# Chunk tables of a scan mixer: products formed in the stored layout instead of being transposed packet by packet

## The reference, cut to what matters

```python
lam_bar = jnp.exp(lam * dt)
b_bar = ((lam_bar - 1.0) / lam)[..., None] * lax.complex(b_re, b_im)
bu = einsum('bsgp,gnp->bsgn', u, b_bar)         # u: [512, 64 groups, 16]
hs = associative_scan(a1*a2, a2*x1 + x2)        # h[t] = lam_bar*h[t-1] + bu[t]
y  = einsum('gpn,bsgn->bsgp', c, hs).real       # forward + backward, + d_skip*u
```

## Time and profile before

| | |
|---|---|
| runs, device time | 2927.89, 2930.91 (median), 2933.01 us |
| profiled execution, its own time | 2930.03 us |
| its span | 2928.2 us |
| PE busy | 2796.3 us, 95% of the span, 15552 products |
| PEld busy | 2277.3 us, 78% |
| DVE busy | 1570.8 us, 54% |
| ACT busy | 1134.6 us, 39% |
| POOL busy | 339.3 us, 12% |
| instructions | 38710 |

### The profile page before, as it was taken

How to read it: one execution, slowest core, us unless ns; L and a number is a source line. 1 busy time by engine, 2 the same in 40 slices (tenths; PEclk the granted TensorE clock), 3 DMA queues, 4 the chain that set the end, 5 groups by cost and what they waited for, 6 DMA issues and landing times. The chain is left out here.

```text
span 2928.2 us, 38710 instructions
## 1 busy us (share of the span) xinstructions
PE 2796.3 (95%) x15552; PEld 2277.3 (78%) x15552; DVE 1570.8 (54%) x2341; ACT 1134.6 (39%) x1792; POOL 339.3 (12%) x426
## 2 busy tenths in 40 slices
PE   9999999599999999999999899999999999999887
PEld 8788888488888877777788578888988888776665
DVE  7776664754434434554535654344654344664656
ACT  5332232364222324645647342223432123543443
POOL 0333221710000001111112300000000000110100
PEclk9999999799999999999999799999999999999989
DMA  4245557554444223222222323222222222211101
GB/s 142 96 147 170 156 155 222 192 160 120 130 127 116 96 75 110 70 92 80 87 94 91 126 101 101 101 88 103 69 101 89 99 100 101 82 49 40 57 15 46
DMA packets 116020, 307.08 MB, mean 105 GB/s; under 512 B 28176, under 2 KB 73808, under 8 KB 87296
## 3 DMA queue, kind: packets, MB, share of 16 engines
q1 hardware_dynamic: 108064, 278.39, 29.0%
q10 hardware_dynamic: 6336, 21.76, 2.1%
q0 software_dynamic: 1440, 4.46, 0.5%
HBM read 266.91 MB, written 41.85 MB: 105 GB/s over the span
## 5 line engine op out<-in xcount | busy, mean ns | idle before, releaser
L94 PE MATMUL ps<-hh_,wh_ 128*128 128x512 f32 x2184 | 867.2, 397 | 8.8 <-DVE hl_ L135 5.1
L94 PE MATMUL ps<-hh_,wl_ 128*128 128x512 f32 x2184 | 853.9, 391 | 0.0
L94 PE MATMUL ps<-hl_,wh_ 128*128 128x512 f32 x2184 | 853.7, 391 | 0.0
L121 DVE TENSOR_TENSOR wl_<-raw_,wh_ 128x2048 fp32r<-128x2048 f32 (+4 forms) x245 | 483.2, 1975 | 503.6 <-ACT wh_ L117 503.1
L117 ACT ACTIVATE wh_<-raw_ 128x2048 fp32r<-128x2048 f32 (+3 forms) x244 | 400.6, 1648 | 351.6 <-PE ps L94 331.2
L94 PEld LDWEIGHTS ps<-hh_,wh_ 128*128 128x128 f32 x2184 | 412.2, 189 | 107.0 <-issue 9.3
L94 PEld LDWEIGHTS ps<-hh_,wl_ 128*128 128x128 f32 x2184 | 411.9, 189 | 87.4
L94 PEld LDWEIGHTS ps<-hl_,wh_ 128*128 128x128 f32 x2184 | 412.4, 189 | 86.2 <-issue 2.9
L94 PE MATMUL ps<-ah_,wh_ 128*128 128x512 f32 x704 | 275.1, 391 | 0.0
L94 PE MATMUL ps<-al_,wh_ 128*128 128x512 f32 x704 | 274.0, 389 | 0.0
L94 PE MATMUL ps<-ah_,wl_ 128*128 128x512 f32 x704 | 274.0, 389 | 0.0
(11 more groups left out here) (363 smaller groups left out, 3584.5 us busy)
## 6 DMA issues: line engine op xcount, KB each, us to landing
raw_<-in_w SPq DMA_DIRECT2D x203, 1024.0 KB, 5.0
sO<-s5ce_ SPq DMA_DIRECT2D x32, 256.0 KB, 3.7
sW<-s5wt_ SPq DMA_DIRECT2D x16, 512.0 KB, 6.0
sA<-os_ SPq DMA_DIRECT2D x24, 256.0 KB, 2.1
ol_<-sA SPq DMA_DIRECT2D x24, 256.0 KB, 3.6
sT<-sK SPq DMA_DIRECT2D x32, 128.0 KB, 4.0
wh_<-sO ACTq DMA_DIRECT2D x4, 1024.0 KB, 6.1
wl_<-sO ACTq DMA_DIRECT2D x4, 1024.0 KB, 7.5
```

The lines of the kernel that those rows point to most:

```text
L94: return self.e.matmul(out, lhsT, rhs, start=start, stop=stop, skip_group_check=True)
L121: return Nothing() if self.e is None else self.e.tensor_tensor(out, a, b, op)
```

## The change

- The eight transposes of every packet go, with the two ACT copies behind them. Instead `P.G` is transposed once (eight transposes, two ACT copies), written to HBM (`sG`, 512 KB), and for each packet eight DMAs of 64 KB spread the packet's powers over the partitions in the layout of sW (`chunk_sync`; in the trace's terms `s5G_<-sG`). One more table from the host (`s5bt`, 512 KB a packet, to `P.bx`, `s5bx_`) has b in that layout. The x = 1 part is then formed from these and goes into `P.wt` as it is stored.
- What PE needs of `wn` for sK are two powers per state only. POOL forms these in six operations of 128x64 for each packet (`scaled_b`), from `P.fb`, a copy of the first power that DVE makes once. PE now waits for `p.wn` in place of `p.f(pc, 1)`.
- A packet takes nine slots in place of eight. DVE starts packet pc in slot 27 + 9pc, PE forms its products in slot 32 + 9pc: packet 13 in slot 149, packets 14 and 15 in what would be slots 158 and 167, past the 153 of FFN 0.

The core of the diff:

```diff
+    for _ in range(PREP_FIRST + 2):
+        yield
+    sp.wait_ge(*K.at("p.gt", 1))
+    sp.dma(d["sG"].rearrange("r b q n -> q (r b) n"), P.flat.rearrange("p (b n) -> p b n", b=8)).then_inc(*K.lane("s5sG").up("p.sG"))
+    yield
+    sp.wait_ge(*K.at("p.w"))
+    sp.dma(P.bx[:, :, :], d["s5bt"][0]).then_inc(*K.lane("s5gx").up())
+    sp.wait_ge(*K.at("p.sG"))
+    chunk_sync(K, sp, 0, range(8))
+    yield
+    for pc in range(16):
+        yield
+        if pc % 4 == 0 and pc:
+            same_sync(K, sp, pc // 4 - 1)
         yield
...
+        sp.wait_ge(*K.at("p.f", pc, 1))
+        sp.dma(d["sW"][un][:, 1024 * hf:1024 * hf + 1024], P.flat).then_inc(*K.lane("s5sW").up("p.sW", pc))
         if pc < 15:
-            sp.wait_ge(*K.at("p.f", pc, 1))
+            sp.wait_ge(*K.at("p.wn", pc))
             sp.dma(P.bc[:, :, :, :], d["s5bc"][pc + 1]).then_inc(*K.lane("s5bc").up("p.bc", pc + 1))
-        yield
-        yield
+            sp.dma(P.bx[:, :, :], d["s5bt"][pc + 1]).then_inc(*K.lane("s5gx").up())
+        yield
+        if pc < 15:
+            chunk_sync(K, sp, pc + 1, range(4))
+        yield
+        if pc < 15:
+            chunk_sync(K, sp, pc + 1, range(4, 8))
         yield
...
+def chunk_sync(K, sp, pc, powers):
+
+    for i in powers:
+        sp.dma(K.prep.G[16 * i:16 * i + 16, :, :, :].rearrange("p r s g -> p r (s g)"),
+               bass.AP(K.d["sG"].tensor, 512 * pc + 8192 * i, [[0, 16], [65536, 2], [1, 512]])).then_inc(
+            *K.lane("s5gx").up(*(("p.gx", pc) if i == 7 else ())))
...
+    for r in range(2):
+        ac.wait_ge(*K.at("p.gp", r))
+        ac.act(P.flat[:, 512 * r:512 * r + 512], K.mb["p.gp", r], ACT.Copy).then_inc(*ac.up("p.gt", r))
+        ac.mark("out", "p.gp", r)
+    yield
+    yield
...
-        yield
-        if pc:
-            ac.wait_ge(*K.at("p.sW", pc - 1))
-        for r in range(2):
-            ac.wait_ge(*K.at("p.t", pc, r))
-            ac.act(P.wt[:, :, r, :], K.mb["p.t", pc, r].rearrange("p (g x) -> p g x", g=4), ACT.Copy).then_inc(*ac.up("p.wt", pc, r))
-            ac.mark("out", "p.t", pc, r)
-        yield
+        for _ in range(4):
+            yield
...
-    for _ in range(4):
+    for _ in range(8):
         yield
     dv.wait_ge(*K.at("p.G"))
+    dv.cp(P.fb[:, :, :], pw[:, :, 0, :]).then_inc(*dv.up("p.fb"))
     for pc in range(16):
         for x in range(2):
-            out = (P.ce, P.wn)[x]
+            out = P.ce[:, 0, :, :, :], P.wt[:, :, 0, :]
...
-            dv.wait_ge(*K.at("p.bc", pc))
+            dv.wait_ge(*K.at(("p.bc", "p.gx")[x], pc))
...
+            if x:
+                dv.wait_ge(*(K.at("p.sW", pc - 1) if pc else K.at("p.sG")))
+            elif pc:
+                dv.wait_ge(*K.at("p.ab", pc - 1))
+                dv.wait_ge(*K.at("p.sO", pc - 1, 1))
...
-            dv.tt(out[:, 0, :, :, :], v[0], v[1], ALU.subtract).then_inc(*dv.up("p.o0", pc, x))
+            dv.tt(out[x], v[0], v[1], ALU.subtract).then_inc(*dv.up("p.o0", pc, x))
...
+def scaled_b(K, po, pc):
+
+    P = K.prep
+    t = [P.t2[:, 512 + 64 * i:576 + 64 * i].rearrange("p (g x) -> p g x", g=4) for i in range(2)]
+    fr, fi = (P.fb[:, r, 4 * pc:4 * pc + 4].rearrange("p (g x) -> p g x", x=1).broadcast_to([128, 4, 16]) for r in range(2))
+    br, bi = P.bc[:, 0, :, :], P.bc[:, 1, :, :]
+    po.wait_ge(*K.at("p.fb"))
+    for r, (x, y, op) in enumerate(((br, bi, ALU.subtract), (bi, br, ALU.add))):
+        po.tt(t[0], x, fr, ALU.mult).then_inc(*po.up())
+        po.tt(t[1], y, fi, ALU.mult).then_inc(*po.up())
+        if r == 0 and pc:
+            po.wait_ge(*K.at("p.ab", pc - 1))
+        po.wait_ge(*po.now())
+        po.tt(P.wn[:, r, :, :], t[0], t[1], op).then_inc(*po.up(*(("p.wn", pc) if r else ())))
+        po.wait_ge(*po.now())
...
 def prep_tensor(K, pe):
     P = K.prep
     ce, wn = P.ce, P.wn
-    for _ in range(PREP_FIRST):
+    for _ in range(PREP_FIRST + 1):
+        yield
+    pe.wait_ge(*K.at("p.G"))
+    for r in range(2):
+        b = K.mb.take("p.gp", r)
+        pe.wait_ge(*K.after(pe, K.mb, "p.gp", r))
+        for i in range(4):
+            m = pe.tr(b[:, 128 * i:128 * i + 128], P.gx[:, r, 128 * i:128 * i + 128], K.ident)
+        m.then_inc(*pe.up("p.gp", r))
+    for _ in range(3):
         yield
     for pc in range(16):
-        for _ in range(6):
+        for _ in range(4):
             yield
...
-        pe.wait_ge(*K.at("p.f", pc, 1))
+        pe.wait_ge(*K.at("p.wn", pc))
         for r in range(2):
             for g in range(4):
                 o = slice(32 * g, 32 * g + 16)
-                pe.mm(ba[o, 0:128], wn[0:64, r, g, 7, :], ce[0:64, r, g, 0:8, :], r == 0, r == 1).then_inc(*pe.up())
-                pe.mm(bb[o, 0:128], wn[64:128, r, g, 0, :], ce[64:128, r, g, 2:10, :], r == 0, r == 1).then_inc(*pe.up())
+                pe.mm(ba[o, 0:128], wn[0:64, r, g, :], ce[0:64, r, g, 0:8, :], r == 0, r == 1).then_inc(*pe.up())
+                pe.mm(bb[o, 0:128], wn[64:128, r, g, :], ce[64:128, r, g, 2:10, :], r == 0, r == 1).then_inc(*pe.up())
         pe.mark("p.ab", pc)
-        yield
-        for r in range(2):
-            b = K.mb.take("p.t", pc, r)
-            pe.wait_ge(*K.after(pe, K.mb, "p.t", pc, r))
-            for g in range(4):
-                m = pe.tr(b[:, 128 * g:128 * g + 128], wn[:, r, g, :, :].rearrange("p s x -> p (s x)"), K.ident)
-            m.then_inc(*pe.up("p.t", pc, r))
-        yield
+        for _ in range(5):
+            yield
...
-    e.wait_ge(*K.at("p.t", 15, 1))
+    e.wait_ge(*K.at("p.ab", 15))
+    e.wait_ge(*K.at("p.f", 15, 1))
     e.wait_ge(*K.at("p.sO", 15, 1))
```

More of the change, by code:

```diff
@@ L933, in prep_sync @@
     sp.dma(P.bc[:, :, :, :], d["s5bc"][0]).then_inc(*K.lane("s5bc").up("p.bc", 0))
-    for _ in range(PREP_FIRST):
+    for _ in range(PREP_FIRST + 2):
         yield
-    for pc in range(17):
-        if pc:
[L938 to L945, removed]
+    sp.wait_ge(*K.at("p.gt", 1))
[7 more added lines that the diff above has]
+    for pc in range(16):
         yield
+        if pc % 4 == 0 and pc:
+            same_sync(K, sp, pc // 4 - 1)
         yield
@@ L988, in prep_scalar @@
     ac.act(u[5], u[1], ACT.Sin, scale=0.5).then_inc(*ac.up("p.s2"))
-    for _ in range(PREP_FIRST - 2):
+    for _ in range(PREP_FIRST):
         yield
+    for r in range(2):
[4 more added lines that the diff above has]
+    yield
     for pc in range(16):
-        for _ in range(6):
+        for _ in range(5):
             yield
@@ L1099, in prep_vector @@
             if x == 0:
-                dv.stt(out[:, 1, :, :, :].rearrange("p g s x -> p (g s x)"), P.t1[:, 0:n], -1.0, P.t2[:, 0:n],
+                dv.stt(P.ce[:, 1, :, :, :].rearrange("p g s x -> p (g s x)"), P.t1[:, 0:n], -1.0, P.t2[:, 0:n],
                        ALU.mult, ALU.subtract).then_inc(*dv.up("p.f", pc, x))
             else:
-                dv.tt(out[:, 1, :, :, :], v[0], v[1], ALU.add).then_inc(*dv.up("p.f", pc, x))
+                dv.tt(P.wt[:, :, 1, :], v[0], v[1], ALU.add).then_inc(*dv.up("p.f", pc, x))
             yield
-        yield
         yield
@@ L1113, in prep_vector @@
         yield
+        yield
+        yield
     yield
 def prep_views(P, pc, x):
[L1118 to L1122, removed]
-    return n, v, er, ei, xr, xi
+    if x:
+        v = [t[:, 0:512].rearrange("p (g n) -> p g n", g=4) for t in (P.t1, P.t2)]
+        tabs = [t[:, r, :].rearrange("p (g n) -> p g n", g=4) for t in (P.gx, P.bx) for r in range(2)]
+        return 512, v, *tabs
+    n = 640
+    v = [t.rearrange("p (g s x) -> p g s x", g=4, s=10) for t in (P.t1[:, 0:n], P.t2[:, 0:n])]
+    er, ei = (P.E[:, r, :, 4 * pc:4 * pc + 4].rearrange("p s (g x) -> p g s x", x=1).broadcast_to([128, 4, 10, 16]) for r in range(2))
+    xr, xi = (P.bc[:, r, :, :].rearrange("p g (s x) -> p g s x", s=1).broadcast_to([128, 4, 10, 16]) for r in (2, 3))
+    return n, v, er, ei, xr, xi
+def scaled_b(K, po, pc):
[12 more added lines that the diff above has]
+        po.wait_ge(*po.now())
 def prep_gpsimd(K, po):
@@ L3839, in _s5 @@
     bc = np.ascontiguousarray(np.stack(b, 1).transpose(2, 0, 1, 3, 4))
+    bt = np.stack(b[:2]).reshape(2, 128, 16, 4, 16).transpose(2, 4, 0, 3, 1).reshape(16, 1, 16, 2, 512)
+    bt = np.broadcast_to(bt, (16, 8, 16, 2, 512)).reshape(16, 128, 2, 512)
     ds = np.zeros((4, 32, 16, 16), np.float32)
@@ L4015, in memory @@
         P.pw = P.ce[:, :, :, :, :].rearrange("p r g s x -> p (r g s x)")[:, 0:1152].rearrange("p (r k g) -> p r k g", r=2, k=9)
-        sm = P.wn[:, :, :, :, :].rearrange("p r g s x -> p (r g s x)")[:, 0:512].rearrange("p (k g) -> p k g", k=8)
-        P.u = [sm[:, i, :] for i in range(8)]
-        P.lr, P.li, P.dt = (P.wn[:, 1, i, :, :].rearrange("p s x -> p (s x)")[:, 0:64] for i in range(3))
+        P.u = [P.bx[:, 0, 64 * i:64 * i + 64] for i in range(8)]
+        P.lr, P.li, P.dt = (P.bx[:, 1, 128 * i:128 * i + 64] for i in range(3))
+        P.gx = P.G[:, :, :, :].rearrange("p r s g -> p r (s g)")
```

(5 more changed lines are left out.)

16 lines of the change are left out of this document (4 added, 12 removed).

## The result

The changed kernel takes 2976.8 us (median of four runs, 2969.4 to 2982.2) beside 2931.0 before: ratio 1.016, interval 1.014 to 1.018. Slower, as forecast, but by 46 us where 19 were forecast, and outside the range. The profiled execution has a span of 2967.6 us, 39.4 more than before. The whole loss arises before the scan: PE's first output product stands at 630.6 us in place of 582.9, +47.7. Some 8 us come back much later, in stretches that the change doesn't touch: of the same work, 1200 to 1300 us had a granted clock of 0.93 before and (47.7 us later) 0.97 after. Such clock differences come and go between executions, and the other three runs lie higher than the profiled one.

The account below looks back on a forecast made before the run. PE was taken to bound FFN 0, a chain of transfers and small operations the part behind it. FFN 0 saves 14.6 less 3 us, yet the first scaled U comes 18.6 later: 2930.0 + 18.6 = 2949 us, range 2937 to 2963.

Parts of the forecast that it names:

- What FFN 0 saves: PE in FFN 0: transposes, two packets' products and stream restarts go, one transpose set comes back; 14.6 us saved.
- What FFN 0 loses: Hold-ups of PE in FFN 0, at the start and through DVE waiting for POOL; 3 us together.
- the second: DVE in FFN 0 stands for POOL's six operations per packet, mostly covered by spare time; 0 to 10 us, 2 taken.
- the first: Start of FFN 0: copies, sG's write, nine DMAs and POOL's operations before packet 0's products; 0 to 5 us, 1 taken.
- What stands behind FFN 0: Packets 14 and 15, then U, from the last add at 478.0 to the first scaled U at 518.3.
- The first parts: x = 0 part of packets 14 and 15: two rounds of POOL's 1.34 and DVE's 0.82 us, 4.6 us.
- The second parts: x = 1 part of packets 14 and 15: POOL's six small operations 2.4 us, then 4.9 us as before.
- the next parameters: Packet 15's parameters, issued by SP behind packet 14's write of sW; 3.5 us taken.
- from packet 15's end to U: 506.7 to 518.3: DVE's operations on `tk` 0.5 us, SP's sK writes 2.09, U's loading 9.
- U or the row sums last: Behind packet 15: row sums end at 513.8 to 519.7, perhaps last by 1.4 us; U at 518.3 taken as later.
- The clock of the first table products: Table products behind longer PE idle may run at the lower clock, at most 5 us; nothing charged.
- the third: Rival: DVE and POOL become the bound in gate and up, FFN 0 no shorter; +10 to +12 us more, 2960; 15%.

Follow-up runs that it names:

- e2: Changed kernel, but POOL's six small operations (powers of b) run for packet 0 alone, left out for packets 1 to 15; 2947.3 us, ratio 1.007.
- e5: Changed kernel with nine slots, POOL's six small operations ahead of each packet's first part in place of ahead of its second; 2952.1 us, ratio 1.007.
- e3: Changed kernel, but the eight chunk DMAs and the load of b in the stored layout are issued for packet 0 alone; 2968.2 us, ratio 1.013.
- e9: Changed kernel, small operations ahead of first part, next parameters loaded behind sO's write, nine slots in gate and up, six in down; 2929.4 us, ratio 1.000.
- e7: Changed kernel with eight-slot packets, small operations ahead of first part, next parameters loaded behind sO's write; 2941.2 us, ratio 1.0035.

## Why the prediction was wrong

The direction and the mechanism that it named for the loss stand: two packets behind FFN 0, with nothing beside them. It missed a second one, which takes back more than FFN 0 saves, and the tail was sized too short. Of its terms:

- **What FFN 0 saves.** 14.6 us forecast. e2, with almost no stalls, has the last add 14.4 us earlier than the kernel before. Right.
- **What FFN 0 loses: this step failed.** It read: "The bound is 0 to 10 us; I take 2" for the second, and 1 for the first, "since PE's products are queued several deep and the trace shows only 0.4 us of such waits so far". Measured 19.7 us (e2 against the change). It took a wait of 0.4 us for the absence of a dependence, but a wait that is nought tells nothing of the slack behind it. In the trace of before, from the end of a packet's last part on DVE to PE's products are 0.2, 0.7, 1.4 and 2.0 us in the first four packets, and 2.6 to 7.6 in the others, at four slots' distance. The tightest is packet 0, whose two rows stand below. The change keeps four slots, from the first part now, and puts at least 2.8 us of POOL into them. In four of the six packets where PE waited, its products stand 3.1 us behind DVE's end, POOL's operations and two gaps of 0.14; in the other two 7.8 and 4.9. The prediction had DVE as the one that would stand for the six operations; PE's own wait for their end (`p.wn`), 10.9 us here, isn't in its sum. The eight waits are 15.1 us, and the stretches at the lower clock behind the three longest of them add some 4, by the distances of the products there. The start, forecast at 1 us, cost nothing: the first wait for `wn` is at 195 us.
- **What stands behind FFN 0.** 40.3 us from the last add to the first scaled U were forecast, 53.2 measured. Of the 12.9 missing, 8.3 are the start: the sum let packet 14 begin 1.4 us behind the last add, its parameters loaded, so it put this wait at nothing; SP had issued them at 490.67 behind 1 MB of writes and beside ACT's table loads, the issue took 4.54 us, and DVE could begin 13.8 us from its start. In e5, where FFN 0 isn't held up, DVE still stands 4.5 us for them. The first parts took 5.9 us in place of 4.6 each (2.7): POOL's operation took 1.97 us when it began together with DVE's, where the sum had 1.34 from a row in which POOL ran alone. The second parts were 7.7 for 7.3 (0.9), the next parameters 4.2 for 3.5 (0.7), and from packet 15's end to U 12.0 for 11.6 (0.4).
- **U or the row sums last.** I left U as the later; the row sums were, at the lower clock, near the upper bound given for them (10.5 of 11.8).
- **The clock of the first table products.** Nothing was charged, and nothing came: 0.79 from 548.0 to 557.3, 0.78 before.

The rows of packet 0 in the trace of before, DVE's last part and PE's products, 0.15 us apart:

```profile
137.38 0.69 DVE L121 TENSOR_TENSOR s5wn_<-s5t_ 128x512 f32<-128x512 f32 x1
138.22 0.66 PE L94 MATMUL ps<-s5ce_,s5wn_ 64*16 64x128 f32 x32 [0.41 <-DVE s5wn_ L121]
```

The last add came 16.9 us later than forecast (494.85 for 478.0), and the part behind it took 12.9 more; with the 18.6 forecast that is the 48.3 us at the first scaled U. Of the rivals, the third had the right sign and place (FFN 0 no shorter than before, last add behind 489) but put 2960 on it, with the tail at its forecast length. Its mechanism holds in small part: DVE was busy 80.86 and POOL 46.38 of 123 us, so neither was full, and the chunk DMAs that came late carried some 6 us (e3).

## What to carry to other kernels

When an operation gets a new producer, measure the slack that the old one had, packet by packet, from its end to its consumer's start; a wait list shows only the slack that is already negative. Small operations on a side engine belong where their own inputs are ready, not behind work and loads that they don't need (e5: 18 us). A number of slots that fits background work in one stage doesn't carry over to another, and neither do its microseconds: 15.8 us a packet all but served in down (e9), and 22.6 did not in gate and up (e7). When a table's last piece moves behind the stage that hid it, look up when its inputs are loaded, and put that wait into the sum.

## What the runs showed of the hardware

In FFN 0 of the changed kernel, each of the three stops of PE by 2.7 to 4.0 us inside a dense stream was followed by some 3 us of products 0.43 us apart in place of 0.23, so that it cost about half as much again; the four stops of 1.0 to 1.5 us were followed by no such stretch. POOL's multiplication of 128x640 took 1.97 us when DVE's 0.83 us began within 0.1 us of it, and 1.34 to 1.35 alone, 0.63 more. The Trainium skill, page "SBUF — State Buffer", section "SBUF: two separate sides", has the port pair that the two share as a lock held for a whole instruction. By that the multiplication would take 1.34 + 0.83 = 2.17 us, an estimate; the 1.97 us measured are 0.2 less, and the measurement decides.

A DMA's issue on SP, 0.5 us in a quiet stretch, took 1.5 (23.24 us for 16) while ACT's 1 MB loads were under way, and 0.7 (11.39 for 16) when four of these were put behind it.
